# Gate panels of an attention layer projected inside the attention instead of ahead of it

## What is computed

```python
def moba_layer(x, pos, w_in, w_out):
    h = x @ w_in                       # 1024 x 4096
    q, k, v, g = _split(h, ODD_SPLITS) # four of 1024
    q = rope(_heads(q, MOBA_HEADS), pos)
    k = rope(_heads(k, MOBA_HEADS), pos)
    o = moba_attention(q, k, _heads(v, MOBA_HEADS))
    return (_merge(o) * jax.nn.silu(g)) @ w_out
```

## Time and profile before

| | us |
|---|---|
| median of three runs (lowest, highest) | 3129.0 (3126.4, 3129.66) |
| span of the profiled execution | 3122.5 |
| TensorE busy in the span | 3014.5 (97%) |
| VectorE busy in the span | 2007.9 (64%) |
| ScalarE busy in the span | 1512.8 (48%) |
| gate panels' products, 2389.3 to 2412.5 | 23.1 |
| block attention, first score to the next stage's first instruction on TensorE | 2413.9 to 2452.0 |

### The profile page before, as it was taken

One profiled execution on the slowest core, in us unless ns is written; L12 is line 12 of the kernel. 1 busy time (PEld: TensorE's weight loads), 2 busy tenths in 40 slices (PEclk: granted clock), 3 DMA queues, 4 the chain that ended last, 5 costly groups with the idle time before them and its releaser, 6 DMA issues. The chain is left out here.

```text
span 3122.5 us, 43115 instructions
## 1 busy us (share of the span) xinstructions
PE 3014.5 (97%) x17959; PEld 2637.2 (84%) x17959; DVE 2007.9 (64%) x2237; ACT 1512.8 (48%) x1692; POOL 24.1 (1%) x41
## 2 busy tenths in 40 slices
PE   7999998899999999999999999999999999999998
PEld 6889897788888899778888888998789798997898
DVE  4547647555455467498898987554555756787755
ACT  4543343334344345477777776443434445432453
POOL 0001000000000000000000000000000000000000
PEclk9999999999999999999999999999999999999999
DMA  5338650065555567599999998541445143345142
GB/s 194 132 124 265 223 185 28 9 242 189 188 189 184 173 211 243 201 361 351 354 363 350 370 349 298 174 145 60 141 167 177 42 162 135 135 152 177 55 169 95
DMA packets 197852, 606.10 MB, mean 194 GB/s; under 512 B 19648, under 2 KB 59401, under 8 KB 154394
## 3 DMA queue, kind: packets, MB, share of 16 engines
q1 hardware_dynamic: 192306, 588.23, 53.0%
q0 software_dynamic: 3872, 12.71, 1.3%
q10 hardware_dynamic: 1480, 2.41, 0.3%
HBM read 602.26 MB, written 1.05 MB: 193 GB/s over the span
## 5 line engine op out<-in xcount | busy, mean ns | idle before, releaser
L2121 DVE TENSOR_TENSOR w_lo<-ring,w_hi 128x2048 fp32r<-128x2048 f32 x336 | 769.7, 2292 | 336.2 <-ACT w_hi L2016 331.0
L2016 ACT ACTIVATE w_hi<-ring 128x2048 fp32r<-128x2048 f32 x336 | 643.1, 1915 | 367.4 <-PE ps L1963 153.4
L358 DVE TENSOR_TENSOR w_lo<-ring,w_hi 128x2048 fp32r<-128x2048 f32 (+2 forms) x209 | 469.4, 2247 | 480.1 <-ACT w_hi L349 479.4
L349 ACT ACTIVATE w_hi<-ring 128x2048 fp32r<-128x2048 f32 (+2 forms) x209 | 392.7, 1881 | 645.1 <-PE ps L470 488.4
L470 PE MATMUL ps<-h_hi,w_hi 128*128 128x256 f32 x1616 | 463.7, 287 | 17.6 <-DVE w_lo L358 10.7
L470 PE MATMUL ps<-h_lo,w_hi 128*128 128x256 f32 x1616 | 459.7, 284 | 0.0
L470 PE MATMUL ps<-h_hi,w_lo 128*128 128x256 f32 x1616 | 459.5, 284 | 0.0
L470 PEld LDWEIGHTS ps<-h_hi,w_hi 128*128 128x128 f32 x1616 | 312.5, 193 | 22.2 <-issue 17.0
L470 PEld LDWEIGHTS ps<-h_lo,w_hi 128*128 128x128 f32 x1616 | 312.6, 193 | 0.3
L470 PEld LDWEIGHTS ps<-h_hi,w_lo 128*128 128x128 f32 x1616 | 312.6, 193 | 0.0
L1926 PE MATMUL ps<-w_hi,h_hi 128*128 128x512 f32 x672 | 266.6, 397 | 1.4 <-DVE w_lo L2121 1.4
(11 more groups left out here) (539 smaller groups left out, 5544.3 us busy)
## 6 DMA issues: line engine op xcount, KB each, us to landing
ring<-in_moe_w_gate_up SPq DMA_DIRECT2D x224, 1024.0 KB, 4.9
ring<-in_moe_w_down SPq DMA_DIRECT2D x112, 1024.0 KB, 4.9
ring<-in_w_in SPq DMA_DIRECT2D x58, 1024.0 KB, 6.9
ring<-in_w_in_even SPq DMA_DIRECT2D x30, 1024.0 KB, 6.9
ring<-in_dense_w_gate_up SPq DMA_DIRECT2D x22, 1024.0 KB, 7.7
ring<-in_w_in_odd SPq DMA_DIRECT2D x16, 1024.0 KB, 6.7
arena<-in_w_ada POOLq DMA_DIRECT2D x24, 512.0 KB, 4.9
ring<-in_b_w_in SPq DMA_DIRECT2D x12, 1024.0 KB, 6.2
```

Of the source, the lines that this page charges most:

```text
L349: k.nc.scalar.activation(self.part(k.w_hi, b, m), src, ACT.Copy).then_inc(k.hi_ready, 1)
L358: k.nc.vector.tensor_tensor(self.part(k.w_lo, b, m), src, self.part(k.w_hi, b, m).bitcast(F32), ALU.subtract).then_inc(k.lo_ready, 1)
L2016: nc.scalar.activation(high(g, h), raw(g, h), ACT.Copy).then_inc(k.hi_ready, 1)
L2121: nc.vector.tensor_tensor(low(g, h), raw(g, h), high(g, h).bitcast(F32), ALU.subtract).then_inc(k.lo_ready, 1)
```

## The change

The gate panels become a job of their own, projected in the attention. Their work is cut into eight blocks: panel q, half h, 128 columns o, each 24 products into one of a fourth pair of banks (6 and 7). The blocks stand behind the scores of iterations 0, 1, 3, 4, 6, 7, 9 and 10. Both panels write the same pair, and each product of the second panel is behind a wait for the first one's eviction. The pair takes the third score bank, so scores take turns on two, and the scores of unit s wait for the exponentials of unit s-2. The 18 identity turns at the start are left out. ScalarE and VectorE round and split the halves at the end of the iterations in which the buffer comes free, and ScalarE evicts the panels with Silu at the ends of iterations 5 and 11. The gate of the first eight units is not there when their outputs are: ScalarE copies these outputs to SBUF, and VectorE multiplies all eight by their gates in one pass at unit 8.

```diff
-    def add(self, runs):
+    def add(self, runs, aside=False):
...
-            self.groups += r.count // r.acc if r.kind not in ("experts", "routed") else 0
+            self.asides += r.count if aside else 0
+            self.groups += r.count // r.acc if r.kind not in ("experts", "routed") and not aside else 0
...
-        m.bank, m.before = group % SLOTS, i + group // SLOTS
+        m.bank, m.before = (SLOTS, r.asides + j) if r.aside else (group % SLOTS, i + group // SLOTS)
...
+class Aside:
...
+    def products(self, pe, s):
+        for (q, h, o), at in zip(self.blocks, self.slots):
+            if at == s:
+                self.stream.products(pe, self.place(q), only=(h, o))
+    def prepare(self, s, split):
+        for j in range(2, 2 * len(self.panels) + 1):
+            if self.slots[2 * (j - 2) + 1] != s:
+                continue
+            if j < 2 * len(self.panels):
+                split(self.place(j // 2), (j % 2,))
+            else:
+                self.stream.first_of_next(split)
+    def evict(self, eng, s, which):
+        for q in range(len(self.panels)):
+            if self.slots[4 * q + 3] + 1 == s:
+                self.stream.evict(eng, self.place(q), which)
...
-    score_banks = (0, 1, 6)
+    score_banks = (0, 1) if aside else (0, 1, 6)
...
-                    if s >= 3:
-                        pe.wait_ge(exp_done, s - 2)
+                    if s >= held:
+                        pe.wait_ge(exp_done, s - held + 1)
...
+                if aside:
+                    aside.products(pe, s)
...
-                    if m == 0:
+                    if m == 0 and not aside:
                         turn_identity(k, 18, 7)
...
+                    if aside and g == late:
+                        aside.all_read(dve)
+                    nc.vector.tensor_tensor(dst, out_of(g), gate, ALU.mult).then_inc(out_read, 1)
+                if is_last and late and g == late:
+                    dst, copied, gate = aside.late_parts
+                    dve.wait_ge(out_copied, late)
+                    nc.vector.tensor_tensor(dst, copied, gate, ALU.mult)
+            if aside:
+                k.stream.open_stage(split)
             for s in range(n_units + 4):
...
+                if aside:
+                    aside.prepare(s, split)
...
+                if aside:
+                    aside.prepare(s, split)
+                    aside.evict(act, s, "act")
...
-           run("T", wo, 2048, k.h, to_tokens(v.v2), count=2),
-           run("F", wo, 3072, k.h, to_features(v.g2, func=ACT.Silu), count=2)])
+           run("T", wo, 2048, k.h, to_tokens(v.v2), count=2)])
+    s.add([run("F", wo, 3072, k.h, to_features(v.g2, func=ACT.Silu), count=2)], aside=True)
...
-    attention(k, "block_attention", groups, v.work2, last_turns=8)
+    beside = Aside(s, [0, 1, 3, 4, 6, 7, 9, 10], 8, (v.cat2[:, 0:4, :], v.cat2[:, 0:4, :], v.g2[:, 0:4, :]))
+    attention(k, "block_attention", groups, v.work2, last_turns=8, aside=beside)
```

More of the change, by code:

```diff
@@ L418, in each_with_next, with products @@
                     step()
-    def products(self, pe, m, by_chunk=False):
+    def products(self, pe, m, by_chunk=False, only=None):
         k, nc, r = self.k, self.k.nc, m.r
@@ L431, in products @@
         for h in range(max(r.parts, 1)):
+            if only and h != only[0]:
+                continue
             kind = r.kinds[h]
@@ L441, in products @@
             for o in range(width // P if kind == "F" else r.tiles):
+                if only and o != only[1]:
+                    continue
                 if r.kind == "R":
@@ L475, in products, with evict @@
                     last = nc.tensor.matmul(out, k.ones_row[0:1, 0:P], row, start=False, stop=True)
-            if h == 0 and r.parts == 2:
+            if h == 0 and r.parts == 2 and (not only or only == (0, 1)):
                 last.then_inc(k.first_half_used, 1)
-        last.then_inc(k.panel_used, 1)
+        if not only or only == (1, 1):
+            last.then_inc(k.panel_used, 1)
+    def evict(self, eng, m, which):
+        k, r = self.k, m.r
+        if r.on == which and m.j % r.acc == r.acc - 1:
+            eng.wait_ge(k.panel_used, m.number + 1)
+            q = m.p if r.acc == 1 else m.j // r.acc
+            r.evict(k.nc, k.ps[:, 2 * m.bank:2 * m.bank + 2, :], q).then_inc(k.group_read[m.bank], 1)
     def stage(self, name, side=None, extra=(), source=(), features=None, norm=False, heads=None,
@@ L1219, with __init__, place, all_read @@
 WHOLE = (0, S)
+class Aside:
+    def __init__(self, stream, slots, late=0, late_parts=None):
+        self.stream, self.slots, self.late, self.late_parts = stream, slots, late, late_parts
+        self.panels = [(r, p) for r in stream.jobs[stream.at] for p in range(r.count)]
+        self.blocks = [(q, h, o) for q in range(len(self.panels)) for h in range(2) for o in range(2)]
+        assert len(slots) == len(self.blocks) and all(r.parts == 2 for r, _ in self.panels)
+    def place(self, q):
+        r, p = self.panels[q]
+        return self.stream.place(r, 0, p)
+    def all_read(self, eng):
+        m = self.place(len(self.panels) - 1)
+        eng.wait_ge(self.stream.k.group_read[m.bank], m.before + 1)
+    def first_read(self, eng):
+        m = self.place(0)
+        eng.wait_ge(self.stream.k.group_read[m.bank], m.before + 1)
+    def products(self, pe, s):
[5 more added lines that the diff above has]
+            if self.slots[2 * (j - 2) + 1] != s:
+                continue
+            if j < 2 * len(self.panels):
[6 more added lines that the diff above has]
+                self.stream.evict(eng, self.place(q), which)
 def unit(scores, values, scale=1.0, mask=None, causal=False, n=S, factor=None, floor=False):
@@ L1236, in unit, with attention @@
     return u
-def attention(k, name, groups, work, last_turns=0, scaled=True):
+def attention(k, name, groups, work, last_turns=0, scaled=True, aside=None):
     nc = k.nc
@@ L1253, in attention, with out_of, gated @@
     diagonals = work[:, 4:6, :].rearrange("p b (t n) -> p b t n", t=TT)
-    score_banks = (0, 1, 6)
+    score_banks = (0, 1) if aside else (0, 1, 6)
+    held = len(score_banks)
+    late = aside.late if aside else 0
+    def out_of(g):
+        _, r0, dv, _, _ = groups[g]
+        return k.ps[r0:r0 + dv, 4 + g % 2, 0:S]
+    def gated(g):
+        return groups[g][4] is not None and g >= late
     with stage(k, name) as st:
@@ L1259, in attention, with _ @@
         values_done, out_read, dve_order = st.sem("values_done"), st.sem("out_read"), st.sem("dve_order")
+        out_copied = st.sem("out_copied") if late else None
         def scores_of(s):
-            return k.ps[:, score_banks[s % 3], :]
+            return k.ps[:, score_banks[s % held], :]
+        if aside:
+            @st.block.sync
+            def _(sp):
+                k.stream.ahead(sp)
         @st.block.tensor
@@ L1411, in _ @@
                     u, g, _, is_last = units[m]
[L1412 to L1413 removed]
+                    if is_last and not gated(g):
+                        dst = groups[g][3]
                         act.wait_ge(values_done, m + 1)
[L1415 removed]
+                        nc.scalar.activation(dst, out_of(g), ACT.Copy).then_inc(out_copied if late else out_read, 1)
+                if aside:
+                    aside.prepare(s, split)
+                    aside.evict(act, s, "act")
+    if aside:
+        k.stream.at += 1
 def swiglu_run(w_gate_up, w_down, experts, ff):
@@ L3855, in build @@
     k.first_half_used = nc.alloc_semaphore("first_half_used")
-    k.group_read = [nc.alloc_semaphore(f"group_read{i}") for i in range(SLOTS)]
+    k.group_read = [nc.alloc_semaphore(f"group_read{i}") for i in range(SLOTS + 1)]
     k.stream = Stream(k)
```

35 lines of the change are left out of this document (18 added, 17 removed).

## The result

The changed kernel takes 3140.93 us (median of four runs, 3140.11 to 3141.07). Beside it the kernel before took 3127.7 (four runs, 3122.53 to 3129.66). The ratio is 1.0051, 95% interval 1.0037 to 1.0064: slower by 12 to 20 us (the two medians lie 13.2 apart). The forecast was 3142.0, 13.0 us slower, and the range 3133 to 3147.

A forecast was written before the change was run, and what follows sets the result against it. In the attention's steady part TensorE and VectorE were both taken as full at about 2.12 us an iteration. Chain +10.1, clock +1.7 and +1.2 make +13.0 on 3129.0: 3142.0 us, range 3133 to 3147.

The forecast's parts named there:

- wait ahead of unit 1's transposes: Attention start: after block 3, TensorE idles 1.0 us because unit 1's scaling stands behind a late VectorE split.
- wait at block 5: Attention middle: TensorE idles 6.4 us until ScalarE evicts the first panel from the bank pair that the second panel reuses.
- wait at values 10: Near the attention's end: TensorE idles 2.7 us for a ScalarE copy behind the second eviction and its table loads.
- the clock: Lower granted clock after the two long TensorE idles in the attention: 1.7 us plus 1.2 us.
- The chain: Attention followed through the in-order queues: last turns at 69.7 us, less 36.6 and 23.0, gives +10.1 us.
- I take 1.2: Clock loss after the 2.7 us idle ahead of values 10: 0 to 1.7 us, taken as 1.2.
- The other signs: Projection 23 us shorter; TensorE idles of 5 to 7 and 2 to 3 us; VectorE waiting 3 to 5 us three times.
- the cross-check: Attention length: 16 iterations of 2.12 and eight blocks of 2.97 are 57.7, idle pieces some 12, together 69.7 us.
- TensorE with room: Attention: TensorE has room that the blocks fill, so not slower; 3115.6 us, or 3122 at half size; chance 0.04.
- Waits mostly hidden: Attention: eviction no later than block 5, so its idle and clock loss go; +2 to +5, 3131 to 3134; chance 0.12.
- A dearer switch: ScalarE in the attention: a table switch costs more than its load, adding 2.4 us, 3144.4 us; chance 0.06.
- That the change doesn't do what it says: Attention: the blocks stay behind each other instead of being interleaved; no size given; chance 0.01.

The follow-up runs named there:

- the first execution: The changed kernel as it is, its first profiled execution: attention 79.8 us; the kernel's median is 3140.93 us.
- the first repeat: The changed kernel as it is, profiled a second time: 3137.07 us, attention 76.4 us.
- turns in the waits: Changed kernel with TensorE turning the identity 50 times ahead of block 5's wait and 22 times ahead of values 10: 3135.8 us, ratio 1.0023.
- the new order: Changed kernel with panels evicted one iteration earlier, ScalarE's roundings one iteration later and VectorE's splits two later: 3128.43 us, ratio 1.0011.
- (split): Changed kernel with VectorE's three splits inside the iterations moved to the end of the next iteration: 3140.55 us, ratio 1.0039.
- (tables): Changed kernel with gate panels evicted by Copy in place of Silu, so without table loads inside the attention: 3137.96 us, ratio 1.0036.
- (eviction): Changed kernel with each gate panel evicted in the iteration of its last block, ahead of the rounding: 3141.41 us, ratio 1.0041.

## Why the prediction was right, and where it was off

| step | forecast, us | measured, us |
|---|---|---|
| projection without the gate panels | -23.0 | -23.0 |
| wait ahead of unit 1's transposes | 1.0 | 1.10 in all three executions |
| wait at block 5 | 6.4 | 6.27, 6.28, 6.28 |
| wait at values 10 | 2.7 | 2.69, 2.70, 2.69 |
| a block at full clock | 2.97 | 2.97 |
| attention's growth without the clock | +33.1 | +33.4 |
| the clock | +2.9 | +8.2, +4.8, +6.8 |

The growth without the clock is worked out from the first execution: the last turns start 78.3 us after the first score, less 8.2 for the clock is 70.0, less 36.6 before. The clock's part is what three stretches took over their length at full clock: block 1 (3.06 in the first repeat; 4.49 only in the first execution), block 5 (2.97), and values 10 to the last turns (9.06 with turns in the waits; 13.81, 12.67 and 13.82 here, so 4.75, 3.6 and 4.76).

**The chain was right**, term by term. The loss is in the order of two queues and in the low clock behind the waits that this order makes: with the order changed, 12 to 20 us become 0.3 to 6.3 (ratio 1.0001 to 1.002). ScalarE's eviction is queued behind a maximum that VectorE takes behind a split that waits for ScalarE's rounding; moving the parts of that chain takes the wait at block 5 from 6.27 to 3.13 (split), to 4.98 (tables), or away (eviction). Those three are read from timelines; as times, only the turns and the new order are clearly shorter than the changed kernel. That TensorE was full at 2.12 us an iteration is shown from two sides: less work on VectorE brings nothing, and with the waits gone the blocks cost 25.2 us. VectorE's 2.11 in the earlier trace rows is from start to start at the common pace and could have held idle time; but its own pace with work queued up, 1.65, and 0.45 for a gate product make 2.10.

**The step that was mis-sized is the clock**, above all "I take 1.2" for the wait at values 10. That figure came from a stretch behind 2.70 us without work in which the granted clock was back soon; behind the same idle in this tail it stayed low for 13.7, 10.2 and 13.7 us and cost 4.75, 3.6 and 4.76. The 1.7 for block 5 came out at 2.1, 1.2 and 2.1, and block 1's 1.4, in the first execution alone, was not forecast. The sentence that a part of the loss would not show there, since VectorE's pace is close to TensorE's, was wrong too: at half the clock an iteration takes 3.88 us, and VectorE needs 2.11. So the whole is worth 4.8 to 8.2, and the attention's growth less 23.0 is +18.7, +15.3 and +17.3 in the three executions, against the 13.0 forecast. The sign "70 to 73 us from first score to last turns" failed with it: they were 78.3, 74.9 and 76.8. The other signs came, VectorE's three waits for ScalarE's rounding among them (3.60, 4.23 and 4.50 us).

**Why the median still fell close:** the attention's growth over the three executions, 40.1 less 23.0, is +17.1 in the mean; the spans differ by 16.0 in the mean (3138.3, 3135.3, 3141.6 against 3122.5 and 3122.4); the medians by 13.2 beside each other and by 14.7 against the later runs of the kernel before (3126.2). Part of the closeness is luck: the forecast's base, 3129.0, lies above the later runs, and its profiled execution (3122.5 and the 1.8 around it) below them. The forecast took 4 to 7 us to lie around the span; it is 1.8 here (3140.11 less 3138.3). The number did not depend on it. Nor did it on the cross-check, whose "some 12" of idle pieces are 11.0 by the chain's own terms (1.0, 6.4, 0.9 and 2.7). The upper end of the forecast's own range, +16, adds up to +16.6.

**Small terms taken as nothing:** the late gating costs 2.2 us by itself in the kernel before; in the changed kernel its two small waits for an output's copy are 0.47 and 0.40 us, the 0.9 that the forecast had. The two score banks by themselves cost no more than the runs can tell (1.0009, from 0.9998 to 1.0019), though the profiled attention was 4.0 us longer. The four moved loads show no wait on TensorE.

**The rivals.** TensorE with room: falls, as above. Waits mostly hidden: falls, all three stand at their forecast lengths. A dearer switch: here the load starts 0.02 us behind the copy and the eviction 0.01 behind the load, and without the load the wait is 1.29 shorter. The Trainium skill ("ScalarE: Activation LUTs", "What ACT_TABLE_LOAD costs") counts 1.38 us of drain besides; no run here shows it, and the measurement decides. That the change doesn't do what it says: the timeline shows it does.

## What to carry to other kernels

Before work is moved beside other work, look at the busy times of the stretch where it goes, not at the program's: here two engines were full at the same pace, and the best order nearly broke even. Then follow each in-order queue past every instruction that is added; worked out from rows of the kernel before, the waits came within 0.13 us. What did not come out is the clock: behind waits like these (2 to 6 us on TensorE), let the range of its price reach to half the length of the stretch that follows (4.75 of 9.06 us here), or fill the wait with turns.

## What the runs showed of the hardware that I had not expected

The lower clock can outlast the wait that brought it by far, although TensorE always has an instruction (busy 13.81 of the tail's 13.81 us): behind 2.0 to 2.7 us without work, the 1.2 GHz level held for 10.2 to 17.1 us in the attention's tail in five executions of three kernels (the changed one, the early eviction, the later split). With turns in the waits, or without the wait, the same tail ran at 2.4 GHz. But the reordered kernel had a wait of 2.05 us just ahead of its tail and stayed at full clock; what makes the difference was not found, and stays open. Stage starts differ as well: behind the same 1.47 us of idle the clock fell for 3.4 us in three kernels' profiled executions and not in others, and not in the repeats of the changed kernel. Single executions of the kernel before spread over some 12 us, and the granted clock goes with it: the shortest of twenty (3120.02 us) has a mean of 0.991, the longest (3132.63) 0.986. Where their low stretches lie is not on record.
